# A hybrid decoder step in twelve stages: the semaphore clears move into the following stage, with one barrier less for each stage, and the seventh square of a norm moves from the first MLP into the odd projection

## The reference

```python
def rmsnorm(x, w):
    xf = x.astype(jnp.float32)
    y = xf * lax.rsqrt(jnp.mean(xf * xf, axis=-1, keepdims=True) + EPS)
    return (y * w.astype(jnp.float32)).astype(x.dtype)
...
        xp = xp + dp
        xs = xs + ds
        xp = xp + sq_relu_mlp(rmsnorm(xp, norm_mlp[layer]), w_up[layer], w_down[layer])
        xs = xs + sq_relu_mlp(rmsnorm(xs, norm_mlp[layer]), w_up[layer], w_down[layer])
```

## Time and profile before

| quantity | value |
|---|---|
| median of 3 executions | 3014.14 us (3011.75 to 3016.54) |
| the profiled execution's own time | 3007.65 us |
| its span from first to last instruction | 3005.8 us |
| TensorE busy | 2889.6 us, 96% of the span |
| VectorE, ScalarE, GpSimd busy | 53%, 40%, 54% of the span |
| mean granted TensorE clock | 0.990 of full |

### The profile page before, as it was taken

How to read it: one execution, slowest core, us unless ns; L and a number is a source line. 1 busy time by engine, 2 the same in 40 slices (tenths; PEclk the granted TensorE clock), 3 DMA queues, 4 the chain that set the end, 5 groups by cost and what they waited for, 6 DMA issues and landing times. The chain is left out here.

```text
span 3005.8 us, 56734 instructions
## 1 busy us (share of the span) xinstructions
PE 2889.6 (96%) x22695; PEld 2655.9 (88%) x22695; DVE 1606.6 (53%) x2238; ACT 1213.1 (40%) x2106; POOL 1637.9 (54%) x1372
## 2 busy tenths in 40 slices
PE   8999999988999999999999999998999999999998
PEld 8998666665677999998999989997799999989997
DVE  3222365555554474447666636635546645476665
ACT  4211435555543343344444352313534443444443
POOL 1122103455541167878999814731111778799994
PEclk9999999999999999999999999999999999999999
DMA  6122205798883134446444144668532444454442
GB/s 193 36 87 69 96 18 189 264 315 287 276 310 123 50 119 152 143 140 217 146 147 139 51 142 142 228 225 306 203 116 62 139 147 146 154 202 139 139 139 81
DMA packets 324854, 471.60 MB, mean 157 GB/s; under 512 B 21521, under 2 KB 222673, under 8 KB 324466
## 3 DMA queue, kind: packets, MB, share of 16 engines
q1 hardware_dynamic: 303858, 383.21, 38.2%
q0 software_dynamic: 19872, 82.46, 7.7%
q10 hardware_dynamic: 864, 2.31, 0.2%
HBM read 342.56 MB, written 125.35 MB: 156 GB/s over the span
## 5 line engine op out<-in xcount | busy, mean ns | idle before, releaser
L151 PE MATMUL mlp_X<-mlp_f_hi,mlp_w_hi 128*128 128x272 f32 x1968 | 568.0, 289 | 9.5 <-DVE xT L973 7.7
L152 PE MATMUL mlp_X<-mlp_f_lo,mlp_w_hi 128*128 128x272 f32 x1968 | 567.5, 288 | 0.0
L153 PE MATMUL mlp_X<-mlp_f_hi,mlp_w_lo 128*128 128x272 f32 x1968 | 566.7, 288 | 0.0
L808 POOL TENSOR_TENSOR mlp_w_lo<-mlp_raw,mlp_w_hi 128x256 fp32r<-128x256 f32 (+1 forms) x348 | 347.0, 1004 | 153.2 <-ACT mlp_w_hi L692 112.1
L151 PEld LDWEIGHTS mlp_X<-mlp_f_hi,mlp_w_hi 128*128 128x128 f32 x1968 | 370.2, 188 | 12.3 <-DVE xT L973 9.3
L152 PEld LDWEIGHTS mlp_X<-mlp_f_lo,mlp_w_hi 128*128 128x128 f32 x1968 | 370.6, 188 | 0.0
L153 PEld LDWEIGHTS mlp_X<-mlp_f_hi,mlp_w_lo 128*128 128x128 f32 x1968 | 370.3, 188 | 0.0
L808 POOL TENSOR_TENSOR mlp_w_lo<-mlp_sums,mlp_w_hi 128x256 fp32r<-128x256 f32 (+1 forms) x276 | 310.0, 1123 | 13.2 <-ACT mlp_w_hi L692 9.9
L151 PE MATMUL mlp_Z<-mlp_f_hi,mlp_w_hi 128*128 128x272 f32 x976 | 281.3, 288 | 3.6 <-ACT mlp_ev L731 2.0
L152 PE MATMUL mlp_Z<-mlp_f_lo,mlp_w_hi 128*128 128x272 f32 x976 | 281.4, 288 | 0.0
L153 PE MATMUL mlp_Z<-mlp_f_hi,mlp_w_lo 128*128 128x272 f32 x976 | 281.1, 288 | 0.0
(11 more groups left out here) (582 smaller groups left out, 7485.6 us busy)
## 6 DMA issues: line engine op xcount, KB each, us to landing
hidden<-mlp_ev SPq DMA_DIRECT2D x224, 272.0 KB, 2.2
mlp_f_lo_plain<-hidden SPq DMA_DIRECT2D x112, 544.0 KB, 5.9
mlp_raw<-in_w_down SPq DMA_DIRECT2D x64, 512.0 KB
mlp_raw<-in_w_up SPq DMA_DIRECT2D x48, 512.0 KB
mla_kd<-in_cache_turned SPq DMA_DIRECT2D x128, 160.0 KB
projections<-odd_zout SPq DMA_DIRECT2D x24, 544.0 KB, 3.8
forms<-gla_f SPq DMA_DIRECT2D x20, 544.0 KB, 2.7
mix_kd_more<-in_cache_turned SPq DMA_DIRECT2D x60, 160.0 KB
```

The costliest lines, as they stand in the source:

```text
L151: pe.matmul(out, w_hi, x_hi, start=first, stop=False, skip_group_check=onto)
L152: pe.matmul(out, w_hi, x_lo, start=False, stop=False, skip_group_check=onto)
L153: return pe.matmul(out, w_lo, x_hi, start=False, stop=last, skip_group_check=onto)
L808: pool.tensor_tensor(to, x, y, op).then_inc(done_by, 1)
```

## The change

`Stage.__exit__` no longer clears its semaphores and has no barrier of its own: it appends them to a list `K.used`. The next stage's GpSimd stream begins with `s.clear_used()`, which clears the list. One barrier is left between two stages, the block's own. The store stage has no GpSimd stream, so what mlp1 and store leave is cleared after the last stage, ahead of one `all_engine_barrier`, the only one left. Since a stage now takes its semaphores while those of the one before are not yet free, the numbers are spread over more ranges: the range clears, each with a drain, rise from 32 to 42.

The square of k = 6 leaves `SquaresAhead` and is made with that of k = 7 in odd: `REST` is now two tiles, with a square and an addition ahead of k = 5 and ahead of k = 6, and a second scratch tile of `G.f`.

```diff
     def __exit__(self, *a):
 
         self.stack.__exit__(*a)
-        self.nc.clear_and_free_semaphores(self.sems)
-        self.nc.all_engine_barrier()
+        self.used += self.sems
+
+    def clear_used(self):
+
+        self.nc.clear_and_free_semaphores(list(self.used))
+        self.used.clear()
...
-    REST = KD - 1
+    REST = (KD - 2, KD - 1)
...
-    def act_square(self, act):
-        act.activation(self.sq, self.K.xT[:, self.REST, :], ACT.Square).then_inc(self.squared, 1)
-
-    def dve_add(self, dve):
-        dve.wait_ge(self.squared, 1)
-        dve.tensor_tensor(self.K.acc[:], self.K.acc[:], self.sq, ALU.add).then_inc(self.added, 1)
+    def act_square(self, act, n):
+        act.activation(self.sq[n], self.K.xT[:, self.REST[n], :], ACT.Square).then_inc(self.squared, 1)
+
+    def dve_add(self, dve, n):
+        dve.wait_ge(self.squared, n + 1)
+        if n:
+            dve.wait_ge(self.added, n)
+        dve.tensor_tensor(self.K.acc[:], self.K.acc[:], self.sq[n], ALU.add).then_inc(self.added, 1)
 
     def pe(self, pe, parts):
         if self.own is None:
-            pe.wait_ge(self.added, 1)
+            pe.wait_ge(self.added, len(self.REST))
...
-                    for k in range(2 * g, min(2 * g + 2, KD - 1)):
+                    for k in range(2 * g, min(2 * g + 2, KD - 2)):
                         act.wait_ge(added, i - STEPS_UP)
...
         @block.gpsimd
         def _(pool):
+            s.clear_used()
...
-            if following is not None:
-                ahead.add(dve, KD - 2)
-
         @block.tensor
...
-                if k == 6:
-                    norm.act_square(act)
+                if k in (5, 6):
+                    norm.act_square(act, k - 5)
                 high(act, k, xhi_done)
...
-                if k == 6:
-                    norm.dve_add(dve)
+                if k in (5, 6):
+                    norm.dve_add(dve, k - 5)
                 dve.wait_ge(xhi_done, k + 1)
...
         store_stage(nc, K)
+        nc.clear_and_free_semaphores(K.used)
+        nc.all_engine_barrier()
```

More of the change, by code:

```diff
@@ L63, with __init__ @@
 class Stage:
-    def __init__(self, nc, name):
+    def __init__(self, nc, name, used):
         self.nc, self.name, self.stack, self.sems = nc, name, ExitStack(), []
+        self.used = used
     def __enter__(self):
@@ L172, in load_stage @@
 def load_stage(nc, K, following, second):
-    with Stage(nc, "load") as s:
+    with Stage(nc, "load", K.used) as s:
         filled = s.sem("filled")
@@ L205, in store_stage @@
 def store_stage(nc, K):
-    with Stage(nc, "store") as s:
+    with Stage(nc, "store", K.used) as s:
         y, sq = s.sb("y", [P, 4, D]), s.sb("sq", [P, D])
@@ L459, in mlp_stage @@
     ON_POOL = [n for n in range(N) if n % 2]
-    with Stage(nc, name) as s:
+    with Stage(nc, name, K.used) as s:
         f_hi, hi_plain = s.sb_twice("f_hi", [P, N, 4, HALF])
@@ L1186, in column @@
         return BASE[GROUPS[g][0]] + GROUPS[g][1] * P
-    with Stage(nc, "even") as s:
+    with Stage(nc, "even", K.used) as s:
         x_hi, x_lo = s.sb("x_hi", [P, KD, T], F32R), s.sb("x_lo", [P, KD, T], F32R)
@@ L1447, in latent_stage @@
         read_at[name] = reads[reader]
-    with Stage(nc, "latent") as s:
+    with Stage(nc, "latent", K.used) as s:
         cq = K.xT[:, 0:3, :]
@@ L1716, in wide_before @@
         return sum(wide(m) for m in range(n))
-    with Stage(nc, "pattn") as s:
+    with Stage(nc, "pattn", K.used) as s:
         p, pT = s.sb("p", [P, 2, SEQ]), s.sb("pT", [P, 2, 8, P])
@@ L1989, in sigmoids_at @@
         return any(2 * step + LEAD - SLOTS * h == 14 for h in range(HEADS))
-    with Stage(nc, "mix") as s:
+    with Stage(nc, "mix", K.used) as s:
         lat = s.sb("lat", [P, RING - M.AHEAD, ROWF])
@@ L2938, in width @@
         return T if n + 1 < LS or n >= K_DEC else SEQ
-    with Stage(nc, "odd") as s:
+    with Stage(nc, "odd", K.used) as s:
         x_hi, x_lo = s.sb("x_hi", [P, KD, T], F32R), s.sb("x_lo", [P, KD, T], F32R)
@@ L2944, in odd_stage @@
         bank = [[s.ps(f"bank{i}{c}", [P, 512]) for c in range(NC)] for i in range(2)]
-        zout, norm = s.sb("zout", [P, ZB, T]), Norm(s, K, G.f[:, 0, :])
+        zout, norm = s.sb("zout", [P, ZB, T]), Norm(s, K, [G.f[:, n, :] for n in range(2)])
         b = G.f[:, DB:DB + HEADS, :]
@@ L3331, in gla_stage @@
         read_at[name] = reads[reader]
-    with Stage(nc, "gla") as s:
+    with Stage(nc, "gla", K.used) as s:
         f = G.f
@@ L3821, in count @@
         return ORDER.index((g, c)) + 1 if g < 2 else 3 * g + c + 1
-    with Stage(nc, "evenout") as s:
+    with Stage(nc, "evenout", K.used) as s:
         x_hi, x_lo = s.sb("x_hi", [P, KD, T], F32R), s.sb("x_lo", [P, KD, T], F32R)
@@ L4068, in odd_out_stage @@
     V = VC * P
-    with Stage(nc, "oddout") as s:
+    with Stage(nc, "oddout", K.used) as s:
         x_hi, x_lo = s.sb("x_hi", [P, KD, T], F32R), s.sb("x_lo", [P, KD, T], F32R)
@@ L4298, in program @@
 def program(nc, K):
+    K.used = []
     with ExitStack() as stack:
```

## The result

The changed kernel takes 2995.86 us in the median of 7 executions (2990.56 to 3004.41), the kernel before 3013.48 us in 7 beside it (3009.07 to 3016.54). The ratio is 0.9947 with a 95% interval from 0.9931 to 0.9963. The forecast had the direction. Its 3003.6 us is 7.7 us too high, and its range began at 2999.0, so the size was missed. The profiled execution took 2995.86 us with a span of 2994.1 us, 11.7 us less than the span before. That is near the 10.55 us of the sum. The two medians differ by 17.6 us, more than the two profiles do, and the experiments ask where that comes from.

What follows compares the result with a forecast made beforehand. TensorE, busy 96% of the span, was taken as the bound, so only its idle stretches could give time. 7.8 + 0 + 0 + 0.4 + 2.35 = 10.55 us off 3014.14 gave 3003.6 us, range 2999 to 3010.5.

Steps and rivals of the forecast that it cites:

- the 10.55 us of the sum: Whole kernel: 7.8 from eight hand-overs, 0 at even and gla, 0.4 at mlp1 to store, 2.35 from the square.
- The second barrier: Between stages: removing it wins the whole release-to-release difference at eight hand-overs, 7.8 us together.
- Load to even: Even's start: the 0.4 us gained is lost waiting at the sums for x; taken as 0.
- odd to gla: Gla's start: VectorE's first copy waits for GpSimd's clears and memset, so the 1.1 us difference is taken as 0.
- the end: mlp1 to store: 0.9 us won, 0.5 lost as mlp1's clears reappear after the last stage; 0.4 net.
- The square: mlp0's end: barrier opens 1.24 instead of 3.59 us behind the small products, 2.35 us won; free in odd.
- The clock: Starts of odd and evenout: granted-clock drops may go; nothing taken, upper ends 0.5 and 1.0 us.
- The base: Whole kernel: profile after at about 2997 us; starting from the runs' median 3014.14 instead, 3003.6 us.
- Absorption: Rival: next waits take half of the 7.8 us, gain 6.6, or 4.3 if the square's returns too; chance 0.15.
- a stall behind the branch: Rival, slower: without the second barrier engines stall on instruction fetch at each hand-over, 11.5 us slower, 3026; chance 0.04.
- The upper case: Clock drops go at odd and evenout, low ends at even and gla won: 12.8 us, 3001.4; chance 0.11.

Runs made afterwards that it cites:

- the barriers alone: Kernel before with only the clears moved and the second barriers removed, the seventh square left in mlp0: 3000.3 us, ratio 0.9964.
- the kernel with three barriers: Changed kernel with three bare all-engine barriers, without clears between them, at the end of each stage: 3009.8 us, ratio 0.9999.
- three pairs at mix's end: Changed kernel with three pairs of small products on TensorE at mix's end, ahead of evenout: 2996.69 us, ratio 0.9952.
- gla's memset first: Changed kernel with GpSimd's memsets in gla moved ahead of its small load and its clears: 2997.0 us, ratio 0.9958.

## Why the direction was right and the size too small

**The second barrier, 7.8 us.** Right. At equal clock the barriers alone bring 8.5 us (1.0 either way); the forecast for them was 7.8 + 0.4 = 8.2. Lengths from a block's release to the next (two profiles of each kernel):

| stage | before | changed | mean change | forecast |
|---|---|---|---|---|
| even | 278.7, 278.9 | 280.3, 278.9 | +0.8 | 0 |
| latent | 69.4, 69.4 | 68.6, 68.6 | -0.8 | -0.8 |
| pattn | 125.2, 125.3 | 123.7, 122.4 | -2.2 | -1.4 |
| mix | 434.8, 434.4 | 431.2, 431.1 | -3.4 | -0.9 |
| evenout | 110.3, 110.3 | 110.6, 111.9 | +1.0 | -1.0 |
| mlp0, with the square | 706.1, 706.1 | 702.7, 703.0 | -3.2 | -3.25 |
| odd | 305.6, 306.8 | 304.4, 304.4 | -1.8 | -0.9 |
| gla | 142.6, 142.7 | 141.1, 141.5 | -1.4 | 0 |
| oddout | 101.1, 101.1 | 100.4, 100.3 | -0.8 | -0.8 |
| mlp1 | 703.0, 702.6 | 702.5, 702.7 | -0.2 | -1.1 |
| store and end | 22.6, 22.6 | 21.9, 21.9 | -0.7 | -0.4 |

Latent, mlp0 and oddout are right to 0.1 us. In pattn and gla the rest is the clock's (above). Even's 280.3 has a granted clock of 0.99, the other three lengths 1.00. Most of odd's miss is the late load in the 306.8 of the kernel before. Mix is within its scatter. Evenout did not get shorter in any profile. In the two here its clock is lower than before, but in two variants of the changed kernel it is 110.6 us long at 0.98 as well, so the clock is only part of the cause and the rest stays open. Mlp1 is an exception of another kind, with 0.2 us less idle where 1.1 was forecast; there one wait for ScalarE was 2.0 us in both profiles before and 2.9 and 2.7 in those of the changed kernel. In two variants of the changed kernel (three pairs at mix's end, gla's memset first) it was 2.0 and 2.1 and mlp1 701.6 and 702.0 us long, so there most of the 1.1 us came.

**Load to even, odd to gla, the end.** Right: 0.4 us turned into wait at even's sums, gla's copy kept its distance of 3.57 us and was on the path, and 0.6 us came back at the end.

**The square, 2.35 us.** Right: 3.59 us went to 1.20, nothing in odd waited for the moved pair, and at equal clock the changed kernel is 2.4 us (1.2 either way) ahead of the barriers alone. Moved by itself it brought 1.2 us.

**The clock.** This step failed: "I take nothing for either, and 0.5 and 1.0 us as upper ends." I looked for drops at two places, worked out what each could give there, and left the rest of the kernel's clock as it was. At odd the bound of 0.5 us held. What the runs showed is a higher clock over the whole execution, 0.9909 for 0.9891, worth 3.2 us, with a gain in gla (0.95 to 0.96, 1.4 us of busy time in the first pair of profiles) and a loss in evenout. What raises it stays open. The time of the kernel with three barriers fits the removed standstill as the cause, but its clock, against its neighbour's, does not settle it. Nor do the runs tell at which hand-overs it comes: the clock of single stages is in the profiles alone, and they scatter by as much.

**The base.** This step failed too, and by as much: "The median of the runs, 3014.14, lies 6.49 above the profiled one, and I take the difference off it: 3003.6 us." Three executions were taken for the level of the kernel, and they lay high: the mean of 93 others is 3010.6, so the base was 3.5 us too high. From there the forecast would have read 3000.1, inside its range, and with the clock's 3.2 us 2996.9, against a mean of 2996.4 measured over 13 executions. The prediction had the better number beside it, "a profile of the changed kernel should come to about 2997"; that execution took 2995.86. That both came so near is in part luck, since single executions of one kernel scatter by some 4 us and the second pair of profiles lay 13.5 us apart.

**The rivals.** Absorption took place at even and gla, as forecast, and partly at mlp1. Of a stall behind the branch no row shows anything: odd's first product starts 0.3 us behind the release. The upper case was nearest in size, but for its parts: its drop at evenout did not go but grew in both profiles.

## What to carry to other kernels

Where all engines stand still between two stages, price the standstill by the events on the queues; here that held to a microsecond in ten. Take the sum off the mean of many executions, not off the median of three. Then compare the granted clock over the whole execution, before and after, since it added 30% to the gain here. And where a stage is longer in one profile than in another, look for a late load before the clock gets the blame, as at odd. And before a wait is priced as gain, shift its cause both ways: gla's copy cost all of a delay and gave nothing when early.

## What was not expected of the hardware

A barrier of all five engines with nothing to wait for costs 0.3 to 0.4 us. With one or two at each stage (0.3 and 0.7 us of standstill) the mean granted clock was 0.9907 and 0.9908, with three (1.0 us) 0.9893; these were measured in three groups, and the clock of the kernel before differed between them by up to 0.0009, so that this is not shown to be the barriers' doing. Mix, with the same products, took 427.4 to 437.4 us in single profiles, at a granted clock of 0.97 to 0.99. The two go together only in part: the longest had 0.97, but the shortest had 0.98. That the second of two barriers cost nothing measurable and the third 8 us stays partly open: 3.9 us of these 8 are the barriers' own length and 2.7 the clock's (0.0015), which leaves 1.6, about the error of the difference. The missing cost of the second, about 4 us, is unexplained.
